# Letting the second gather, the second weights and the prompt's rows wait in the opening of a one-core decoder step

## The reference, cut to what matters

```python
past_cmp = cache_cmp[page_table].reshape(b_, -1, 2, KV_HEADS, HEAD_DIM)   # 8 sequences, 2 MB each

def compress(rows, w1, w2, pe):          # once for keys (w_cmpk1), once for values (w_cmpv1)
    chunks = rows[...].reshape(b_, n_chunks, CMP_STRIDE, KV_HEADS, HEAD_DIM)
    part = jnp.einsum('bcsgd,rsdh->bcrgh', chunks, w1)
    hid = jnp.einsum('rsd,rsdh->h', pe.reshape(CMP_RATIO, CMP_STRIDE, HEAD_DIM), w1)   # the "bias"
    for r in range(CMP_RATIO):
        hid = hid + part[:, r:r + n_cmp, r]
    return jax.nn.silu(hid) @ w2
```

## Time and profile before

| what | value |
|---|---|
| median of 3 runs | 1414.58 us (1412.7 to 1417.36) |
| the profiled execution: its own time | 1417.36 us |
| its span, first to last instruction | 1415.5 us |
| PE busy, share of the span | 1380.0 us, 97% |
| DVE, ACT, POOL busy | 621.8, 518.9, 545.4 us |
| DMA | 151.72 MB, mean 107 GB/s; in the opening the engines are full for stretches |

### The profile page before, as it was taken

One profiled execution on the slowest core, in us unless ns is written; L12 is line 12 of the kernel. 1 busy time (PEld: TensorE's weight loads), 2 busy tenths in 40 slices (PEclk: granted clock), 3 DMA queues, 4 the chain that ended last, 5 costly groups with the idle time before them and its releaser, 6 DMA issues.

```text
span 1415.5 us, 27171 instructions
## 1 busy us (share of the span) xinstructions
PE 1380.0 (97%) x11535; PEld 1326.6 (94%) x11535; DVE 621.8 (44%) x949; ACT 518.9 (37%) x803; POOL 545.4 (39%) x274
## 2 busy tenths in 40 slices
PE   7999999999999999999989999998999999999998
PEld 6999899999999999999756589998999999999997
DVE  4677333330042477548477721115834240033352
ACT  5676622221122222123467743323343431122221
POOL 4330344453344444442034434444444453344440
PEclk9999999999999999999999999999999999999999
DMA  8531122341233352243434433322222332222311
GB/s 300 206 120 60 60 90 89 104 134 60 62 93 101 112 198 89 91 121 93 150 136 180 150 90 90 89 89 90 90 90 91 98 128 81 78 89 89 111 38 60
DMA packets 116419, 151.72 MB, mean 107 GB/s; under 512 B 4646, under 2 KB 111370, under 8 KB 114244
## 3 DMA queue, kind: packets, MB, share of 16 engines
q1 hardware_dynamic: 113820, 117.17, 26.0%
q0 software_dynamic: 2304, 33.56, 6.3%
q10 hardware_dynamic: 232, 0.09, 0.0%
HBM read 147.05 MB, written 7.95 MB: 109 GB/s over the span
## 4 chain that ended last, share of the span: by engine, by line
PE 94%; DVE 3%; ACT 2%; issue 1%; DMA 0%; SPq 0%; ACTq 0%; DVEq 0%
PE bank L1682 76%; PE bank L1624 7%; PE bank L1558 5%; PE bank L1808 1%; ACT sm L906 1%; PE bank L1576 1%; PE bank L1835 1%; PE bank L1864 1%; PE bank L1891 1%; DMA w<-w_cmpk 0%; PE bank L1879 0%; DVE sm L1372 0%; PE bank L1918 0%; ACT yr L1025 0%; PE bank L1844 0%
## 5 line engine op out<-in xcount | busy, mean ns | idle before, releaser
L597 POOL TENSOR_TENSOR wlo<-raw,whi 128x1024 fp32r<-128x1024 f32 (+3 forms) x181 | 457.0, 2526 | 654.4 <-ACT whi L721 654.0
L721 ACT ACTIVATE whi<-raw 128x1024 fp32r<-128x1024 f32 (+3 forms) x182 | 196.2, 1080 | 669.2 <-PE bank L1682 663.0
L1682 PE MATMUL bank<-xh,whi 128*128 128x260 f32 x2016 | 408.1, 284 | 0.4 <-DVE vcS L1051 0.4
L1682 PE MATMUL bank<-xh,wlo 128*128 128x260 f32 x2016 | 407.4, 284 | 0.0
L1682 PE MATMUL bank<-xl,whi 128*128 128x260 f32 x2016 | 407.0, 284 | 0.0
L1682 PEld LDWEIGHTS bank<-xh,whi 128*128 128x128 f32 x2016 | 312.0, 189 | 1.4 <-DVE vcS L1051 0.5
L1682 PEld LDWEIGHTS bank<-xh,wlo 128*128 128x128 f32 x2016 | 312.1, 189 | 0.0
L1682 PEld LDWEIGHTS bank<-xl,whi 128*128 128x128 f32 x2016 | 311.3, 189 | 0.0
L1134 DVE TENSOR_TENSOR tmp<-bank,rr 128x520 f32<-128x520 f32 x88 | 61.5, 699 | 284.1 <-PE bank L1682 283.7
L1682 PE MATMUL bank<-hh,wlo 128*128 128x260 f32 x704 | 141.6, 282 | 0.0
L1682 PE MATMUL bank<-hl,whi 128*128 128x260 f32 x704 | 141.5, 282 | 0.0
(11 more groups left out here) (330 smaller groups left out, 1747.6 us busy)
## 6 DMA issues: line engine op xcount, KB each, us to landing
raw<-ffn_w_gate SPq DMA_DIRECT2D x22, 1024.0 KB, 5.4
raw<-ffn_w_up SPq DMA_DIRECT2D x22, 1024.0 KB, 5.3
raw<-w_mix_in SPq DMA_DIRECT2D x17, 1024.0 KB, 5.3
raw<-ffn_w_down SPq DMA_DIRECT2D x8, 1536.0 KB, 6.6
raw<-ffn_w_down SPq DMA_DIRECT2D x8, 1280.0 KB, 5.8
GB<-state_win_kv SPq DMA_DIRECT2D x8, 512.0 KB, 5.6
raw<-w_mix_out SPq DMA_DIRECT2D x4, 1024.0 KB, 5.2
win_kv_sample<-state_win_kv SPq DMA_DIRECT2D x1, 4088.0 KB
```

Source lines behind the costliest of these rows:

```text
L597: pool.tensor_tensor(tile(wlo, w, k, u), raw_tile(u), tile(whi, w, k, u).bitcast(F32), ALU.subtract)\
L721: act.activation(dst, src, ACT.Copy).then_inc(hi_done, 1)
L1682: ins = pe.matmul(acc(g)[:, h, :], w[:, u % WS, c, :], x[:, c, h * HT:(h + 1) * HT], start=(c == 0 and n == 0), stop=(c == k - 1 and n == 2))
```

## The change: three waits and a split loop

Three waits are added. POOL issues the gather of sequence 1 only after that of sequence 0 has landed; SP issues the value weights only after that landing as well, and the prompt's rows only after the gather of sequence 1 has landed. On PE the 16 bias products of the keys are made in two halves, eight ahead of tiles 0 to 3 and eight behind them.

```diff
             for k, n in enumerate(("k", "v")):
+                if k:
+                    sp.wait_ge(xc_loaded[0], 16)
                 sp.dma_start(w1[:, k, :, :], a[f"w_cmp{n}1"][0]...).then_inc(w1_loaded[k], 16)
             for k, n in enumerate(("k", "v")):
                 sp.dma_start(w2[:, k, :], a[f"w_cmp{n}2"][0]).then_inc(w2_loaded, 16)
+            sp.wait_ge(xc_loaded[1], 16)
             sp.dma_start(xr[:, :, :], a["x_prompt"][0]...).then_inc(x_loaded, 16)
...
             for b in range(2):
+                if b:
+                    pool.wait_ge(xc_loaded[0], 16)
                 gather(XC[b], 0, b, xc_loaded[b])
...
-            def hidden_bias(k):
+            def hidden_bias(k, rows=range(16)):
                 pe.wait_ge(w1_loaded[k], 16)
-                for j in range(16):
+                for j in rows:
...
-            hidden_bias(0)
+            hidden_bias(0, range(8))
             for n in range(4):
                 turn_rows(n)
+            hidden_bias(0, range(8, 16))
```

## The result

The changed kernel's median is 1418.59 us (1416.01 to 1421.5, 12 runs) against 1415.67 us (1412.7 to 1417.57, 12 runs) before, measured side by side: ratio 1.0022, 95% interval 1.0012 to 1.0032, or 3.1 us longer by that ratio (1.7 to 4.5 by the interval). The forecast was 2.6 us longer. The profiled execution took 1421.5 us, the longest of the 12, with a span of 1419.7, 4.2 us more than the profile before.

What follows compares the result with a forecast made beforehand. The value weights' landing was taken to bound the opening through ACT and DVE: first() +0.1 us, swallowed by the later bound, and value weights +2.6 us, on the median of 1414.58 make 1417.2 us, range 1412.8 to 1420.5.

Steps and rivals of the forecast that it cites:

- The bound: Opening: the value weights' landing at 23.39 us sets the first block's end through ACT and DVE; later landings shift it nearly fully.
- the hole on PE: PE's idle 1.74 us ahead of first() at 22.18, ended by DVE's low part of the key tiles; the split fills it.
- When the first rows land: First gather's landing: 15.3 us instead of 15.70, since the value weights no longer share the engines with it.
- rival A: Opening gets shorter: first rows land at 13.1, first() starts 1.75 us sooner, weights don't bind; 1412.8 us, chance 0.07.
- PE ahead of first(): PE before the first block: a 1.9 us wait for rows replaces the 1.74 us hole; first() at 22.3 against 22.18.
- The value weights: Their transfer, issued at 15.4 and sharing the engines with the second gather, lands at 26.0 instead of 23.39, 2.6 us late.
- From there on: ACT, DVE and PE behind the landing: PE waits 1.7 us at tile 8; value bias at 35.6 instead of 33.04.
- The size: Whole kernel: value weights add 2.6 us at the value bias; 1417.2 us on the median of 1414.58.
- rival B: Value bias and the step behind it: TensorE's clock falls, 2.6 us more; +5.2, 1419.8 us; B and beyond 0.18.
- the other way that the prediction left open: Value bias: should the clock not fall at 35.4 us, up to 3 us come back.
- Everything behind keeps its pace: Work behind the value bias runs as before, so the 2.6 us there reach the end.
- POOL and SP: POOL's low part of the key weights ends at 21.1, hidden by 1.2 us; prompt's rows leave SP at about 24.5, not reaching PE.

Runs made afterwards that it cites:

- The undone wait: The changed kernel without SP's wait ahead of the value weights, the other two waits and the split kept; ratio 0.9990 to the kernel before.
- the longer wait: The changed kernel with SP's wait ahead of the value weights set on the second gather's landing instead of the first's; ratio 1.0055 to the kernel before.
- ACT's new order: The changed kernel with ACT's copies of tiles 4 to 7 ahead of the high part of the value weights; ratio 1.0003 to the kernel before.
- the filled wait: Changed kernel without SP's value weights wait, ACT copying tiles 4 to 7 before their high part, ten idle identity products ahead of tile 0; ratio 1.0024.
- the bias inside the steps: Changed kernel without SP's wait ahead of the value weights, with two value bias products after each of the first block's eight steps; ratio 1.0030.

## Why the prediction was right

**The bound.** The prediction put it at the landing of the value weights, not at the hole on PE. The undone wait (0.9990), the longer wait (1.0055) and the waits alone (1.0018) show it from three sides, and the profile of ACT's new order shows the way by which it acts.

**When the first rows land.** Said 15.3, measured 14.58: without the weights beside it the gather won 1.1 us, not 0.4. The four kernels with the weights early have it back at 15.6 to 15.8, with the second gather held back in each, so the share that it had lost was that of the weights. Its late start, of which rival A made something, stayed: with neither of the other issues out, its bytes still come no sooner than 8 us.

**PE ahead of first().** Said 22.3, measured 20.55: the wait for the rows was 1.26 us, not 1.9, and the second half of the bias took 2.26, not 3.48. Where the clock rose later it was 21.4 to 21.8. As forecast, none of it was won at the end.

**The value weights.** Said 26.0, measured 25.88, and 25.3 to 25.7 in the other profiles with this wait. That the sum came so near is luck: two errors cancel, an issue 0.7 us sooner and a transfer of 11.2 us instead of 10.6. Its course was another one, too. The queues from 16 to 20 us:

```profile
q1 hardware_dynamic: 426, 0.87, 80.8%
q0 software_dynamic: 16, 0.26, 18.6%
```

The second gather's bytes came later than said, so the weights had 0.87 of their 1.05 MB by 20 us, where 0.25 MB was said for 18.4; the rest crawled beside the gather, and it was the gather that landed last, at 27.3.

**From there on.** High part, copies, low parts and tile 8 came within 0.2 us of the times given (28.0, 29.3 and 30.7 said; 27.83, 29.12 and 30.66 measured). The value bias was said for 35.6; it came at 35.2 to 35.4 in three profiles with this wait, and at 37.21 in the first one of the changed kernel.

**The size.** 2.6 us was said, 3.1 measured (1.7 to 4.5 by the interval). The term that the sum left out was the clock in PE's wait, which was rival B, given 0.18. B's place was the value bias; in the first profile the lower level came earlier, in the steps and turns from tile 8 on, because PE reached tile 8 at 26.1 and not at 29.0 and waited 4.6 us and not 1.7. In the second profile the wait was 1.24, as the forecast has it, and the other way that the prediction left open came: the clock stayed up in the bias and gave back 1.6 of 2.3 us. "Everything behind keeps its pace" held in two of the four profiles with this landing (2.2 us at the bias and 2.2 at the opening's end). So the nearness of 2.6 and 3.1 is in part luck, and how much of the median comes from the clock no run shows.

**POOL and SP.** POOL's low part of the key weights was in time (20.45 against the block's start at 20.55, so with 0.1 us left instead of 1.2). In the run with ACT's new order PE did wait for it, 0.69 us. The prompt's rows went out at 27.33, not 24.5, since the second gather landed so late; they and the sample's rows kept POOL waiting for 2.20 us, and nothing came of it, as the kernel without that wait shows.

## What to carry to other kernels

Here the transfer that was queued early and crawled beside two gathers landed at 23.4, beside one at 18.3, and held back at 25.9: the wait for a landing added an issue and 1 to 2 us in which the engines stood empty, and holding back the smaller packets did not help them, since they met the next gather. Before holding a transfer back, follow its own landing to who waits for it next, through the order of the engine that consumes it: here four tiles that had nothing to do with the weights stood behind them on ACT. Where PE waits longer in the middle of dense work, price the steps behind the wait at the lower clock too: behind 4.6 and 9.05 us the granted clock here was 0.50, behind the waits of 0.7 to 1.2 us ahead of tile 8 it stayed at 1.00. And where two executions of one program differ by 3.4 us in the stretch that is studied, take a second profile before reading a difference of that size.

## What was not expected of the hardware

The granted clock reads 1.00 from 10 us to its first fall in each of these profiles, yet at first the identity products of 128 columns take 0.22 us each (0.11 later), and a step of six products and a turn 2.13 us (1.14 later). The upper pace came at a moment that differed between executions: at 18 to 22 us in some, and at 25, 26, 27, 28 and, with one-column products among the steps, 34 in others. Until then the column does not tell the level; the pace of like products does. From its first fall on the two agree, as in the filled wait (0.50 and the lower pace up to 26 us). The Trainium skill (TensorE: Matmul & The Clock Gate, section Seeing it yourself) warns that the recorded clock events have been found unreliable on trn2 and should not be fully trusted one by one; these rows agree.

Behind the opening the same work takes a different time from one profile to the next. From the opening's end to the span's end it is 1252.6 us in the profile before and 1252.7 in the changed kernel's first, 1249.9 in its second, 1251.4 with ACT's new order, 1257.3 with that order and the weights early, and 1257.5 with the bias inside the steps. The stretch from 690 to 700 us, in the attention stage, in the kernel before and in the last of these:

```profile
690.00:700.00 10.00, 9.12 (x91) 6.27 (x89) 4.43 (x9) 5.75 (x13) 0.00 (x0) 1.00 0.38 109
```

```profile
690.00:700.00 10.00, 9.41 (x45) 9.00 (x44) 1.25 (x2) 2.50 (x5) 0.00 (x0) 0.51 0.37 110
```

The clock fell to its lower level at about 686 us there, and at about 705 in the kernel before; from 680 to 726 us it stood at that level for some 20 us against some 10. The kernel with ACT's new order and the weights early shows the same course (0.50 from 690 to 700). In the profiles of these two kernels, the two with a ratio of 1.003, this makes up the time beyond what their openings lost (0.9 and 1.1 us). Why most of their runs take 1420 us or more, and whether each such run has this fall, is open; no run here was made for it.
